# Reordering ScalarE, VectorE and GpSimd around a gated linear recurrence in a four-mixer kernel on one core

## The reference, cut to what matters

```
x = rmsnorm(h, final_norm)                    # end of the first block
h = rms_norm(x, norm_pre[0])                  # start of the second
u = h @ w_in; xb, gate = u[:, :1536], u[:, 1536:]
xb = causal_depthwise_conv(xb, conv_w, conv_b)          # 4 taps
r = sigmoid(blockwise(xb, w_a) + b_a)                   # 16 blocks of 96 x 96
i = sigmoid(blockwise(xb, w_x) + b_x)
log_a = -8 * r * softplus(-lam);  a = exp(log_a)
bt = sqrt(-expm1(2 * log_a)) * (i * xb)
h_t = a_t * h_{t-1} + bt_t                              # along the tokens
y = h * silu(gate);  o = y @ w_out
x = x + rms_norm(o, norm_post[0])
```

## Time and profile before

| | |
|---|---|
| three runs, median | 2349.1 us (2347.91 to 2349.46) |
| the profiled execution | 2346.45 us |
| its span, first to last instruction | 2344.7 us |
| TensorE busy | 2230.0 us, 95% of the span |
| VectorE, ScalarE, GpSimd busy | 1214.4, 802.6, 544.3 us |
| mean granted clock of TensorE | 0.982 |
| chain that ended last: TensorE, VectorE, ScalarE, GpSimd | 85%, 8%, 2%, 2% |

### The profile page before, as it was taken

How to read it: one execution, slowest core, us unless ns; L and a number is a source line. 1 busy time by engine, 2 the same in 40 slices (tenths; PEclk the granted TensorE clock), 3 DMA queues, 4 the chain that set the end, 5 groups by cost and what they waited for, 6 DMA issues and landing times.

```text
span 2344.7 us, 26703 instructions
## 1 busy us (share of the span) xinstructions
PE 2230.0 (95%) x10598; PEld 1790.5 (76%) x10598; DVE 1214.4 (52%) x1986; ACT 802.6 (34%) x1337; POOL 544.3 (23%) x355
## 2 busy tenths in 40 slices
PE   7999999998999999999999999999798879999997
PEld 6788886886788888876668888887576757877876
DVE  4666456565744433455457444334958575443342
ACT  3334332433332322233433322222466223323321
POOL 2533234140511101223224110034045031100100
PEclk9999999999999999999999999999999999999999
DMA  4222222221233333232212333322222222222322
GB/s 141 82 71 74 81 81 60 67 72 55 82 97 94 97 99 99 90 109 73 73 64 91 98 99 98 93 97 85 77 90 81 80 69 81 86 77 77 99 72 72
DMA packets 84155, 198.27 MB, mean 85 GB/s; under 512 B 7216, under 2 KB 44208, under 8 KB 84032
## 3 DMA queue, kind: packets, MB, share of 16 engines
q1 hardware_dynamic: 81408, 189.62, 25.6%
q10 hardware_dynamic: 2624, 6.93, 0.9%
HBM read 194.40 MB, written 2.13 MB: 84 GB/s over the span
## 4 chain that ended last, share of the span: by engine, by line
PE 85%; DVE 8%; issue 2%; ACT 2%; POOL 2%; DMA 1%; DVEq 0%; SPq 0%; POOLq 0%; ACTq 0%
PE PS L541 50%; PE PS L585 5%; PE PS L587 5%; PE PS L586 5%; PE PS L610 2%; PE PS L611 2%; PE PS L612 2%; PE PS L1060 2%; PE PS L658 1%; PE PS L668 1%; PE PS L682 1%; PE PS L913 1%; PE PS L903 1%; DVE WL L1654 1%; ACT WH L1095 1%
## 5 line engine op out<-in xcount | busy, mean ns | idle before, releaser
L1654 DVE TENSOR_TENSOR WL<-WR,WH 128x1024 fp32r<-128x1024 f32 x353 | 483.1, 1375 | 736.2 <-ACT WH L1095 735.3
L1095 ACT ACTIVATE WH<-WR 128x1024 fp32r<-128x1024 f32 x353 | 370.7, 1055 | 703.5 <-DMA WR<-in_ws 692.3
L541 PE MATMUL PS<-XH,WH 128*128 128x512 f32 x1024 | 403.1, 394 | 13.0 <-ACT XH L1104 12.7
L541 PE MATMUL PS<-XL,WH 128*128 128x512 f32 x1024 | 399.4, 390 | 0.0
L541 PE MATMUL PS<-XH,WL 128*128 128x512 f32 x1024 | 399.2, 390 | 0.0
L541 PEld LDWEIGHTS PS<-XH,WH 128*128 128x128 f32 x1024 | 192.9, 188 | 57.6 <-issue 14.3
L585 PE MATMUL PS<-XH,WH 128*128 128x512 f32 x544 | 223.9, 412 | 5.3 <-DVE WL L1654 3.7
L541 PEld LDWEIGHTS PS<-XL,WH 128*128 128x128 f32 x1024 | 192.8, 188 | 41.2 <-issue 1.7
L541 PEld LDWEIGHTS PS<-XH,WL 128*128 128x128 f32 x1024 | 192.8, 188 | 40.4
L587 PE MATMUL PS<-XH,WL 128*128 128x512 f32 x544 | 215.3, 396 | 0.0
L586 PE MATMUL PS<-XL,WH 128*128 128x512 f32 x544 | 214.4, 394 | 0.0
(11 more groups left out here) (320 smaller groups left out, 3758.3 us busy)
## 6 DMA issues: line engine op xcount, KB each, us to landing
WR<-in_ws SPq DMA_DIRECT2D x281, 512.0 KB, 3.5
WR<-in_ws SPq DMA_DIRECT2D x144, 256.0 KB, 3.3
B_CB<-gates ACTq DMA_DIRECT2D x8, 512.0 KB, 3.8
XTOK<-in_x SPq DMA_DIRECT2D x2, 1024.0 KB, 8.0
out<-OUT SPq DMA_DIRECT2D x4, 512.0 KB, 2.6
R_D<-in_decay ACTq DMA_DIRECT2D x4, 256.0 KB, 2.6
GAIN<-in_post ACTq DMA_DIRECT2D x1, 512.0 KB, 5.4
CST<-in_cst SPq DMA_DIRECT2D x1, 320.0 KB, 3.2
```

Source lines behind the costliest of these rows:

```text
L541: mm = pe.matmul(PS[:, bank + o, :], l, r, start=first and kk == 0 and i == 0, stop=last and kk == 1 and i == 2)
L1095: nc.scalar.activation(WH[:, s, :], WR[:, s, :], ACT.Copy).then_inc(hi_ready, 1)
L1654: tt(WL[:, s, :], WR[:, s, :], WH[:, s, :].bitcast(F32), ALU.subtract).then_inc(lo_ready, 1)
```

## The change

It has four parts, all within the passage that the section above describes.

1. *Weighted squares.* ScalarE computes `Square(gain * R)` into `L_SG`, tiles 0 to 3 behind the fourth copy to `XH`, tiles 4 to 7 behind the eighth. GpSimd's multiplication by the squared gain (line 1600) goes; it adds ScalarE's tile instead.
2. *First sigmoids.* In the third round of the convolution, ScalarE does `gate_sigmoids(0)` ahead of the four copies `conv_high(8)` to `conv_high(11)`, and `decays(0)` between the second and the third of them. In all rounds the four `last_tap` calls stand together ahead of the copies and splits.
3. *Third root.* `gate_sigmoids(3)` and the split of unit 30 stand ahead of `energy_root(2)`, where they stood behind it.
4. *Splits between the last outputs.* ScalarE splits unit 36 ahead of `recurrent_high(2)`; VectorE splits unit 36 ahead of `outputs(2)`, unit 37 ahead of `outputs_lows(2)`, and units 38 and 39 inside `first_output`. Before, all of them stood behind `first_output` (a reciprocal, line 2087, and eight multiplications, line 2091).

```diff
@@ ScalarE, high half of R
                 nc.scalar.activation(XH[:, k, :], R[:, k, :], ACT.Copy, scale=GV[:, 1, k:k + 1]).then_inc(x_hi, 1)
+                if k % 4 == 3:
+                    for n in range(k - 3, k + 1):
+                        if n >= 4:
+                            act.wait_ge(sq_sum, 28 + 2 * max(n - 4, 1))
+                        c = VEC["final"] + n
+                        nc.scalar.activation(L_SG[:, n % 4, :], R[:, n, :], ACT.Square, scale=VC[:, c:c + 1])\
+                            .then_inc(sq_gain, 1)
@@ ScalarE, convolution
             for j in range(3):
-                last_tap(4 * j)
-                last_tap(4 * j + 1)
+                for o in range(4):
+                    last_tap(4 * j + o)
+                if j == 2:
+                    split(u + 18)
+                    gate_sigmoids(0)
                 for o in range(4):
                     split(u + min(4 * j + 9 + o, 18))
                     conv_high(4 * j + o)
-                    if o < 2:
-                        last_tap(4 * j + 2 + o)
-            gate_sigmoids(0)
-            decays(0)
+                    if j == 2 and o == 1:
+                        decays(0)
@@ ScalarE, recurrence
             split(u + 30)
-            energy_root(2)
             gate_sigmoids(3)
             split(u + 31)
+            energy_root(2)
             decays(3)
...
             out_sigmoids(2)
+            split(u + 37)
             recurrent_high(2)
@@ GpSimd, sums of squares, for each k
-                nc.gpsimd.tensor_tensor(first[:, :], R[:, k, :], R[:, k, :], ALU.mult).then_inc(sq_mul, 1)
-                pool.wait_ge(sq_mul, n + 1)
-                nc.gpsimd.tensor_tensor(second, first[:, :], GV[:, 0, k:k + 1].to_broadcast([P, T]), ALU.mult)\
-                    .then_inc(sq_mul, 1)
+                square = SQT if k else SQS
+                nc.gpsimd.tensor_tensor(square[:, :], R[:, k, :], R[:, k, :], ALU.mult).then_inc(sq_mul, 1)
                 if k:
+                    pool.wait_ge(sq_mul, 32 + k + 1)
                     nc.gpsimd.tensor_tensor(SQS[:, :], SQS[:, :], SQT[:, :], ALU.add).then_inc(sq_sum, 1)
-                    pool.wait_ge(sq_mul, n + 2)
-                    nc.gpsimd.tensor_tensor(L_X[:, 1, :], L_X[:, 1, :], L_X[:, 2, :], ALU.add).then_inc(sq_sum, 1)
+                    pool.wait_ge(sq_gain, k + 1)
+                    so_far = L_SG[:, 0, :] if k == 1 else L_X[:, 1, :]
+                    nc.gpsimd.tensor_tensor(L_X[:, 1, :], so_far, L_SG[:, k % 4, :], ALU.add).then_inc(sq_sum, 1)
@@ VectorE, first_output
                 for k in range(DT):
+                    if k % 4 == 0:
+                        split(U["LO"] + 7 + k // 4)
                     c = VEC["final"] + k
                     r_inc(stt(R[:, k, :], R[:, k, :], VC[:, c:c + 1], L_X[:, 0, :], ALU.mult, ALU.mult))
@@ VectorE, end of the recurrence
             split(u + 36)
             out_inputs(2)
+            split(u + 37)
             outputs(2)
+            split(u + 38)
             outputs_lows(2)
             first_output()
```

More of the change, by code:

```diff
@@ L436, in program @@
         front_done, front_used, v_half, r_part = sem("front_done"), sem("front_used"), sem("v_half"), sem("r_part")
-        z_step, gate_done = sem("z_step"), sem("gate_done")
+        z_step, gate_done, sq_gain = sem("z_step"), sem("gate_done"), sem("sq_gain")
         spread_ready, ms_ready, mg_step, w_diff, w_exp, w_ready = (
@@ L1488, in _, with squares @@
         def _(pool):
-            def squares(s, src, ready, i=None):
+            def squares(s, src, ready, i=None, before=None):
                 i = s if i is None else i
+                before = 8 * i if before is None else before
                 for k in range(DT):
@@ L1501, in squares @@
                     nc.gpsimd.tensor_tensor(SQT[:, :], src[:, k, :], src[:, k, :], ALU.mult).then_inc(sq_mul, 1)
-                    pool.wait_ge(sq_mul, 8 * i + k + 1)
+                    pool.wait_ge(sq_mul, before + k + 1)
                     nc.gpsimd.tensor_tensor(SQS[:, :], SQS[:, :], SQT[:, :], ALU.add).then_inc(sq_sum, 1)
@@ L1588, in _ @@
             pool.wait_ge(stat_done, 4)
-            pool.wait_ge(gv_ready, 1)
             for k in range(DT):
                 pool.wait_ge(r_done, 32 + k + 1)
[L1592 to L1595, removed]
                 if k >= 2:
-                    pool.wait_ge(sq_sum, m)
-                nc.gpsimd.tensor_tensor(first[:, :], R[:, k, :], R[:, k, :], ALU.mult).then_inc(sq_mul, 1)
-                pool.wait_ge(sq_mul, n + 1)
-                nc.gpsimd.tensor_tensor(second, first[:, :], GV[:, 0, k:k + 1].to_broadcast([P, T]), ALU.mult)\
-                    .then_inc(sq_mul, 1)
+                    pool.wait_ge(sq_sum, 28 + 2 * k - 2)
+                square = SQT if k else SQS
+                nc.gpsimd.tensor_tensor(square[:, :], R[:, k, :], R[:, k, :], ALU.mult).then_inc(sq_mul, 1)
                 if k:
+                    pool.wait_ge(sq_mul, 32 + k + 1)
                     nc.gpsimd.tensor_tensor(SQS[:, :], SQS[:, :], SQT[:, :], ALU.add).then_inc(sq_sum, 1)
-                    pool.wait_ge(sq_mul, n + 2)
-                    nc.gpsimd.tensor_tensor(L_X[:, 1, :], L_X[:, 1, :], L_X[:, 2, :], ALU.add).then_inc(sq_sum, 1)
+                    pool.wait_ge(sq_gain, k + 1)
+                    so_far = L_SG[:, 0, :] if k == 1 else L_X[:, 1, :]
+                    nc.gpsimd.tensor_tensor(L_X[:, 1, :], so_far, L_SG[:, k % 4, :], ALU.add).then_inc(sq_sum, 1)
             def out_gates(j):
@@ L1631, in _ @@
             out_gates(2)
-            squares(7, R, residual(6), 6)
+            squares(7, R, residual(6), 6, 40)
             for h in range(RH):
```

## The result

The changed kernel takes 2327.41 us (median of four executions, 2325.19 to 2329.11) against 2349.28 for the kernel before beside it (2347.91 to 2352.11): a ratio of 0.9908, 95% interval 0.9895 to 0.9922. It is 0.9% faster; 2330 was predicted.

The account below looks back on a forecast made before the run. TensorE, 95% of the span, was taken as the bound, with 39.5 us of waits and about 9 us of slow matmuls addressable. Gains of 4.0 + 2.5 + 12.5 = 19.0 us gave 2330 us; range 2319 to 2339 (8 in 10).

Parts of the forecast that it names:

- before's 3.2: At the norm: VectorE's reads of GpSimd's sums were taken to start 3.2 us behind the first sum, as before.
- a new stall of 5.6 at product 1: Before the fifth result of block product 1: TensorE arrives at 1724.0, is let go at 1729.6, waiting 5.6 us.
- energy(0) 3.4 us earlier: On VectorE behind the third convolution round: energy(0) starts at 1713.2 instead of 1716.63, only 3.4 us earlier.
- The turns: VectorE instructions reading two SBUF tensors and GpSimd's instructions alternate, one at a time; those reading PSUM are left free.
- 10 to 13: Behind each longer TensorE stall: some 10 to 13 matmuls start every 0.427 us instead of 0.227, costing 2.0 to 2.8 us.
- stalls of 5.5, 1.5 and 0.8: TensorE waits forecast before unit 29 (5.5 us), unit 30 (1.5 us) and unit 36 (0.8 us).
- about 9 us: Slow matmuls behind TensorE's stalls in the changed passage: about 9 us that the change can address, besides the waits.
- no new stalls: Rival, chance 0.15: turns between VectorE and GpSimd cost little, each engine finds gaps; total gain 35 us, 2314 us.
- given back in full: Rival, chance 0.17: held copies leave energy(0) where it was, stall before unit 29 is longer; gain 11 us, 2338 us.
- The squares are late: Rival, chance 0.05: ScalarE's squares or turns hold GpSimd to 1629, the weighted squares give nothing; 2334 us.
- nothing measurable: Rival, chance 0.04: VectorE's chain to the last low half stays as long, early wins are lost before unit 36; 2346 to 2349.
- Slower: Rival, chance 0.03: VectorE, starved in the third convolution round, passes lateness on; ten GpSimd turns start energy(0) at 1740; 2357.

Follow-up runs that it names:

- the second profile of the changed kernel: The changed kernel, unchanged, executed again under the profiler: 2326.43 us median, ratio 0.9901 to the kernel before.
- the kernel with the early unit splits: The changed kernel with VectorE's splits of units 29, 30 and 31 one place earlier each in its order: 2329.61 us, ratio 0.9922.

## Why the prediction was right, point by point

**Part 1** (forecast 4.0). From GpSimd's tile 4 to TensorE's third result of the next product it took 29.98 us before (to 1634.91) and takes 25.02 after (to 1630.89), 5.0 less. GpSimd's last addition and its wait came as worked out:

```profile
1611.20 1.30 POOL L1610 TENSOR_TENSOR L_X<-L_X,L_SG 128x512 f32<-128x512 f32 x1 [2.59 <-ACT L_SG L1300]
...
1625.38 1.28 POOL L1610 TENSOR_TENSOR L_X<-L_X,L_SG 128x512 f32<-128x512 f32 x1
```

It waits 2.59 us for the first of ScalarE's second four squares, and TensorE waits 0.35 us for the last sum. The term was undersized in one place: VectorE's reads of the two sums start 2.0 us behind the first of them (1628.74 against 1626.72), where I kept before's 3.2. Those 3.2 were read behind sums in part at the lower clock; now the sums run at the full one. The window from 1625.5 to 1631.0, with a granted clock of 1.00 where before has 0.69 (columns as there):

```profile
1625.50:1631.00 5.50, 4.36 (x15) 2.30 (x14) 3.94 (x4) 1.67 (x3) 1.17 (x1) 1.00 0.27 95
```

Alone, the part gave 4.0 by the medians.

**Part 2** (forecast 2.5, with 6.7 us left at product 0, a new stall of 5.6 at product 1, energy(0) 3.4 us earlier). Measured 6.81 and 4.92. Energy(0) started 81.7 us behind the norm's release of TensorE (1634.91 to 1716.63) and now 77.1 (1630.89 to 1707.98): 4.6 earlier, 3.5 in the second profile of the changed kernel. The turns are those of the forecast, instruction for instruction. VectorE in the changed kernel:

```profile
1692.84 2.92 DVE L2133 TENSOR_TENSOR CL<-L_XC,CH 128x512 fp32r<-128x512 f32 x1 [4.67 <-ACT CH L1322]
1695.68 8.01 DVE L2127 SCALAR_TENSOR_TENSOR L_XC<-L_XR,VC,L_XC 128x512 f32<-128x512 f32 x3
...
1707.98 1.75 DVE L2148 SCALAR_TENSOR_TENSOR L_W<-L_W,L_R 128x1536 f32<-128x1536 f32 x1
```

and GpSimd:

```profile
1691.71 3.50 POOL L1623 TENSOR_TENSOR L_W<-CH,CL 128x1536 f32<-128x1536 f32 x1 [65.04 <-PE PS L994]
1695.28 3.85 POOL L1627 TENSOR_TENSOR L_I<-L_I,L_W 128x1536 f32<-128x1536 f32 x1
1699.21 3.08 POOL L1630 TENSOR_TENSOR L_W<-L_A 128x1536 f32<-128x1536 f32 x1
```

A subtraction of 0.69 us takes 2.92: it ends at 1695.76, when GpSimd's first instruction (to 1695.21) has let it run. Three taps take 8.01 us instead of 2.47: one waits for GpSimd's second instruction, one for its third. VectorE's ten instructions take from 1692.84 to 1707.98, 15.1 us, of which 7.8 are the three lost turns. From that same release to GpSimd's recurrence of j = 1 it took 102.96 us before (to 1737.87) and takes 98.67 after (to 1729.56), 4.3 less; 2.6 in the second profile. What differs between the two is how many matmuls run slowly behind the stalls (last section), which I had as 10 to 13 for each.

**Parts 3 and 4** (forecast 12.5 together, with stalls of 5.5, 1.5 and 0.8). From GpSimd's recurrence of j = 1 to the end of the passage: 168.61 us before, 155.58 after, 13.0 less (13.1 in the second profile). The stalls are 4.90, 1.48 and 0.50. The place of the turns, on GpSimd and then on VectorE:

```profile
1772.10 3.94 POOL L1623 TENSOR_TENSOR L_W<-CH,CL 128x1536 f32<-128x1536 f32 x1
```

```profile
1772.61 5.05 DVE L2148 SCALAR_TENSOR_TENSOR L_W<-L_W,L_R 128x1536 f32<-128x1536 f32 x1
1777.58 4.45 DVE L1660 TENSOR_TENSOR WL<-WR,WH 128x1024 fp32r<-128x1024 f32 x1
...
1783.73 5.88 DVE L2157 TENSOR_TENSOR_SCAN L_H<-L_A,L_I 128x512 f32<-128x512 f32 x3
```

Energy(2) takes 5.05 us for 1.75 of work, the split of unit 29 4.45 for 1.2, and the scans wait for GpSimd's last instruction, as I had taken them to do without a row that showed it: 5.88 against 3.46 alone. I had also left instructions that read PSUM out of the turns, and rightly: the four gate inputs of j = 1, with one input in PSUM, take 2.48 us while GpSimd's third instruction of j = 2 runs (1761.12 to 1764.73), the same as in rows 7, where GpSimd is idle until 1729.74.

```profile
1762.26 2.48 DVE L2141 TENSOR_TENSOR L_G<-PS,RB 128x512 f32<-128x512 f32 x4
```

One point of the forecast was a matter of luck. It let GpSimd go ahead of energy(2), though by its own figures VectorE was ready first (1780.80 against 1780.9). With VectorE first, the same turns give unit 29's split at 1787.2 and a stall of about 2 us there instead of 5.5 (an estimate from the forecast's own terms). In the trace GpSimd is ahead by 0.5 us (1772.10 against 1772.61). The sum hardly rests on this order: with energy(2) first, in the run that holds GpSimd back, the stall moved on to unit 30 and the time stayed.

The Trainium skill (GPSIMD Engine Reference, Specifications) says that a VectorE instruction with two SBUF inputs contends with GpSimd. A scan has two, and the trace agrees by these 2.4 us. I hadn't used the Trainium skill's page SBUF — State Buffer (section "SBUF: two separate sides"), which states that the shared pair of ports is an exclusive lock held for the whole of an instruction, with the other engine fully blocked. It speaks for the turns, and the trace agrees: 4002 ns for a tap of 750.

**The sum.** 5.0 + 4.3 + 13.0 = 22.3 us in the profiled execution, and 20.6 in the second (5.0, 2.6 and 13.1, rounded); forecast 19.0, and 21.9 by the medians. No step failed; the terms were small by 1.0 (the read of the sums), 0.1 to 1.8 (a stall of 4.9 instead of 5.6, and the slow matmuls) and 0.5. By the stalls: TensorE's waits up to unit 36 fell from 39.5 us to 21.0, where 23.3 was forecast. The three heads of rows 1 give 39.2 of the 39.5; the rest is a wait of 0.35 for the norm. The slow matmuls behind stalls fell from 30 to 17 in the first profile and to 28 in the second, so they gave 2.6 us or next to nothing where 3 was forecast, and the "about 9 us" of them was too much: 30 at 0.2 us each are 6. In the rivals: *no new stalls* falls with the 4.92 and 4.90 us, *given back in full* with an energy(0) 3.5 to 4.6 us earlier. *The squares are late* and *nothing measurable* fall with part 1 and with unit 36. *Slower* needed ten turns where there are three.

What stays open: whether the parts together give somewhat more than their sum, since the 22.3 and 20.6 us of two profiles lie as far apart as the answer.

## What to carry to other kernels

Where VectorE and GpSimd take turns, cost a moved instruction as a list of turns. Here each short VectorE instruction with two SBUF inputs that met a long one of GpSimd took up to that one's length more (4.00 us instead of 0.75 beside one of 3.85). Two cures gave time: work of VectorE moved into a gap ahead of GpSimd's (5 us), and on top of it an instruction of GpSimd's moved to ScalarE (3 us more). Delaying GpSimd gave nothing. A stall that is removed shows its worth only at the next wait behind it, so follow the chain on the other engines to the last place that they hold TensorE (here unit 36) and ask whether it moved.

## What the runs showed of the hardware that was not expected

The number of matmuls that run at the lower clock behind a stall is not a constant of the stall. In the changed kernel's first profile, those whose starts are 0.427 us apart instead of 0.227 are 6, 5 and 6 behind the stalls of 6.8, 4.9 and 4.9 us; in its second, with the same stalls, 12, 8 and 8. Counted in the same way the kernel before has 9, 9 and 12; the 10 to 13 of the prediction count the first matmul too. The granted clock just behind the first stall, first profile:

```profile
1686.20:1692.20 6.00, 5.93 (x19) 4.80 (x20) 1.89 (x2) 3.05 (x7) 0.49 (x1) 0.71 0.00 0
```

and second:

```profile
1686.60:1692.60 6.00, 5.98 (x14) 4.73 (x15) 1.89 (x2) 2.39 (x4) 0.00 (x0) 0.50 0.00 0
```

The Trainium skill (TensorE: Matmul & The Clock Gate, section "What's actually happening") says that the number of matmuls at the lower clock at the start of a kernel varies from run to run of the same kernel, 6, 11 or 14 in its case. Behind stalls inside this kernel the two profiles agree, with 6 and 12. 0.50 is the lower level, 1.2 GHz, for the whole window; 0.71 is a mix of the two, and 20 weight loads fit in where 15 did. At 0.2 us each, 11 slow matmuls more are 2.2 us, about the difference of the two passages (1.7, with 0.4 us less of stalls in the second). So single profiles of one kernel differ by some 2 us here for this reason alone, and a term of that size can't be read from one of them. In this passage, over all twelve profiles, the stalls of 4.9 us and more were followed by 5 to 13 slow matmuls, and those of 1.1 to 2.8 us by none. The one between them, 3.5 us in the kernel with the early unit splits, was followed by four intervals at the full clock and then by eight slow ones.
